# Feed-forward pass 0 of a hybrid decoder layer as one group of 1024 tokens

## The reference

```
hn2 = rmsnorm(x, norm2_g[l])
up, ffn_new = causal_dwconv(hn2 @ w_up[l], st_ffn[l], ffn_conv_w[l])
a_f, b_f = jnp.split(up, [D_FF], axis=-1)
x = x + (jax.nn.silu(a_f) * b_f) @ w_down[l]
y = rmsnorm(x, norm_f_g)
```

## Time and profile before

| | us |
|---|---|
| median of 3 timed runs | 3282.44 (3282.36 to 3284.39) |
| the profiled execution | 3280.0 |
| its span in the profile | 3278.3 |
| PE busy | 3182.3 |
| DVE busy | 2029.8 |
| ACT busy | 833.8 |
| POOL busy | 566.3 |
| feed-forward part, from PE's first product to the end | 1617.51 to 3278.3 |
| pass 1's first product | 2421.73 |

### The profile page before, as it was taken

The page is one execution under the profiler, slowest core; times in us unless marked ns, Lnnn a source line. Parts: engine busy times, 40 slices in busy tenths (PEclk is TensorE's granted clock), DMA queues, the critical chain, the costliest instruction groups (busy, mean ns, idle before and its releaser), DMA issues.

```text
span 3278.3 us, 56605 instructions
## 1 busy us (share of the span) xinstructions
PE 3182.3 (97%) x22353; PEld 2089.5 (64%) x22353; DVE 2029.8 (62%) x4678; ACT 833.8 (25%) x1743; POOL 566.3 (17%) x929
## 2 busy tenths in 40 slices
PE   7899999999999999996799999999998999999998
PEld 3555565566655565554577777777766766777765
DVE  1566665655566665665556666666675566666668
ACT  1223333233223333233321112211232221222213
POOL 1111110111111111112231111121053112111110
PEclk9999999999999999997799999999999999999999
DMA  7022222222222212215521111111133111111112
GB/s 241 11 82 85 85 65 85 85 64 66 66 78 85 85 66 84 80 54 162 168 80 39 52 52 39 39 52 39 39 124 117 39 52 41 50 39 39 43 35 78
DMA packets 223188, 236.37 MB, mean 72 GB/s; under 512 B 14204, under 2 KB 167332, under 8 KB 222931
## 3 DMA queue, kind: packets, MB, share of 16 engines
q1 hardware_dynamic: 222931, 232.81, 22.4%
HBM read 203.10 MB, written 29.67 MB: 71 GB/s over the span
## 4 chain that ended last, share of the span: by engine, by line
PE 49%; POOL 1%; issue 0%; DVE 0%; ACT 0%; DVEq 0%; POOLq 0%
PE mlp_bank L2131 32%; PE mlp_bank L2205 15%; PE mlp_bank L2219 2%; POOL acc L2453 0%; PE mlp_bank L2211 0%; POOL acc L2458 0%; DVE mcv L2573 0%; DVE acc L2634 0%; PE mlp_bank L2230 0%; ACT mcv L2294 0%; PE mlp_bank L2217 0%; ACT raw L2323 0%; ACT mth L2308 0%; DVE raw L2517 0%; POOL cf L2415 0%
## 5 line engine op out<-in xcount | busy, mean ns | idle before, releaser
L695 PE MATMUL mixer_bank<-arena,hnt 128*128 128x451 f32 x2048 | 864.1, 553 | 16.3 <-DMA arena<-in_w_in_dram 8.3
L2131 PE MATMUL mlp_bank<-arena,ws 128*128 128x256 f32 (+1 forms) x2816 | 648.3, 383 | 9.3 <-ACT raw L2321 9.3
L2131 PEld LDWEIGHTS mlp_bank<-arena,ws 128*128 128x128 f32 x2816 | 536.0, 190 | 92.6 <-ACT raw L2321 10.1
L695 PEld LDWEIGHTS mixer_bank<-arena,hnt 128*128 128x128 f32 x2048 | 366.1, 191 | 306.4 <-issue 301.4
L2205 PE MATMUL mlp_bank<-arena 128*128 128x512 f32 x1120 | 494.2, 593 | 0.0
L2606 DVE TENSOR_TENSOR acc<-acc,mlp_bank 128x512 f32<-128x512 f32 x560 | 370.2, 685 | 55.4 <-PE mlp_bank L2205 54.6
L2205 PEld LDWEIGHTS mlp_bank<-arena 128*128 128x128 f32 x1120 | 213.1, 190 | 234.7 <-issue 205.6
L645 POOL TENSOR_TENSOR ex<-dtt,level 128x512 f32<-128x512 f32 (+1 forms) x114 | 142.9, 1254 | 936.0 <-DVE dtt L1641 637.6
L2573 DVE SCALAR_TENSOR_TENSOR mcv<-raw,cf,mcv 128x512 f32<-128x512 f32 (+2 forms) x352 | 265.4, 770 | 59.2 <-ACT mcv L2294 50.3
L2131 PE MATMUL mlp_bank<-arena 128*128 128x256 f32 (+1 forms) x1056 | 249.4, 386 | 5.3 <-PEq L2716 4.3
L729 PE MATMUL mixer_bank<-wo,th 128*128 128x512 f32 x512 | 248.6, 608 | 2.7 <-DMA wo<-in_w_out_dram 2.1
(11 more groups left out here) (368 smaller groups left out, 3570.3 us busy)
## 6 DMA issues: line engine op xcount, KB each, us to landing
wo<-in_w_out_dram SPq DMA_DIRECT2D x260, 256.0 KB, 2.8
arena<-in_w_up_dram SPq DMA_DIRECT2D x44, 512.0 KB, 4.9
wu<-in_w_up_dram SPq DMA_DIRECT2D x44, 512.0 KB, 4.9
arena<-in_w_down_dram SPq DMA_DIRECT2D x40, 512.0 KB, 4.0
arena<-in_w_in_dram SPq DMA_DIRECT2D x7, 1804.0 KB, 16.2
xc<-in_x_t_dram SPq DMA_DIRECT2D x16, 512.0 KB, 4.1
xt<-in_x_prompt_dram SPq DMA_DIRECT2D x16, 512.0 KB, 5.0
xr<-in_x_prompt_dram SPq DMA_DIRECT2D x16, 512.0 KB, 3.8
```

The lines of the kernel that those rows point to most:

```text
L695: x = pe.matmul(bank[ring(g)][0:N, 0:GW], hnt[:, k, 0:N], w[:, k, g * GW:(g + 1) * GW], start=(k == 0), stop=(k == KT - 1))
L2131: x = pe.matmul(out[:, 0:N], left[:, k, :], xb[:, slot, k, g * N:(g + 1) * N], start=first and k == 0, stop=k == HK - 1, skip_group_check= ...
```

## The change

Pass 0 becomes one group of 1024 tokens. Its products have 512 columns. The run bank now alternates by block in pass 0 (`run_of`). `xb` slots are filled accordingly: the four early loads take the token columns in another order. All x sums of the whole width are needed by the first group, and `first_x_sums` moves to the head of POOL's queue. The convolution keeps pieces of 512 tokens, but both pieces of a block come behind the block's products, and on DVE behind the adds of the down half; on ACT the tanh of piece 0, the first taps of piece 1 and the tanh of piece 1 stand behind the copy of product 1 of the next block. In the last block of pass 0 piece 0 stands between the 7th and the 8th of the 14 adds. `half_block` counts pieces, `group` counts groups. Pass 1 does what it did.

```diff
-                    c0 = 2 * N0 * g + N0 * part
+                    c0 = 2 * N0 * part + N0 * g
...
-        PASSES = ((0, 2, 256, 0, 8), (T // 2, 2, 264, 8, 9))
-        J0 = (0, 2 * FT)
+        PASSES = ((0, 1, 512, 0, 8), (T // 2, 2, 264, 8, 9))
+        J0 = (0, FT)
+        WIDTH = (512, 528)
...
+        def run_of(ps, p, g):
+            return run_bank[g if ps else p]
...
-                    elif fixed(f, 1) and g == 1:
+                    elif fixed(f, 1):
                         pe.wait_ge(s_x1_made, 1)
...
                         m1_out(ps, f, p, 0)
                         if not fixed(f, 1):
-                            tanh(ps, f - 1, G - 1)
+                            if ps == 0:
+                                tanh(ps, f - 1, 0)
+                                first_taps(ps, f - 1, 1 - p, 1)
+                            tanh(ps, f - 1, 1)
...
+            first_x_sums()
             gp.memset(ident[:, :], 0.0).then_inc(s_ident_made, 1)
...
                     weight_sums(ps, 0, 0)
                     x_sums(ps)
-                else:
-                    first_x_sums()
...
-                return lambda: conv(ps, f, e, G - 1, 2 * p + e, i)
+
+                def rest(first=0 if ps == 0 else 1, last=2):
+                    for g in range(first, last):
+                        conv(ps, f, e, g, 2 * p + e, i)
+                return rest
...
-                last = up(ps, i, p, 0, (((), act_part), (first, second)))
+                last = up(ps, i, p, 0, (((), act_part), (first, second)) if ps else ((act_part + first, second),))
...
-                down(ps, i - 1, 1)
-                last()
+                if closing and ps == 0:
+                    down(ps, i - 1, 1, 0, 21)
+                    last(0, 1)
+                    down(ps, i - 1, 1, 7, 28)
+                    last(1, 2)
+                else:
+                    down(ps, i - 1, 1)
+                    last()
```

More of the change, by code:

```diff
@@ L2013, in two_before, with convolved @@
             if fixed(f, 2):
+                return 0 if ps == 0 else FT - 1 + f
+            return group(ps, f - 1, 0)
+        def convolved(ps, f):
+            if fixed(f, 2):
                 return 0 if ps == 0 else 2 * (FT - 1 + f)
-            return J0[ps] + PASSES[ps][1] * (f - 1)
+            return half_block(ps, f - 1, 0)
         def sums(engine, p, s_step, step, s_made):
@@ L2150, in up @@
                     J = group(ps, f, g)
-                    run = run_bank[g % 2]
+                    run = run_of(ps, p, g)
                     if g == 0:
@@ L2272, in m1_out @@
                 J = group(ps, f, g)
-                if g == 0 and two_before(ps, f) is not 0:
-                    act.wait_ge(s_act_made, two_before(ps, f))
+                if g == 0 and convolved(ps, f) is not 0:
+                    act.wait_ge(s_act_made, convolved(ps, f))
                     act.wait_ge(s_tails_kept, FT * ps + f - 1)
                 act.wait_ge(s_m1, J + 1)
-                act.copy(raw[p][0][:, c0:c0 + N], run_bank[g % 2][:, 0:N]).then_inc(s_m1_out, 1)
+                act.copy(raw[p][0][:, c0:c0 + N], run_of(ps, p, g)[:, 0:N]).then_inc(s_m1_out, 1)
             def first_taps(ps, f, p, g):
-                _, G, N, _, _ = PASSES[ps]
-                J = group(ps, f, g)
-                c0 = 2 * N * g
-                sample = ps == 1 and g == G - 1
-                n = 2 * N - S if sample else 2 * N
+                J = group(ps, f, g if ps else 0)
+                c0 = WIDTH[ps] * g
+                sample = ps == 1 and g == 1
+                n = WIDTH[ps] - S if sample else WIDTH[ps]
                 if g == 0:
@@ L2549, in conv @@
             def conv(ps, f, p, g, a, i):
-                _, G, N, _, _ = PASSES[ps]
-                J = group(ps, f, g)
-                c0 = 2 * N * g
-                sample = ps == 1 and g == G - 1
-                n = 2 * N - S if sample else 2 * N
+                J = group(ps, f, g if ps else 0)
+                K = half_block(ps, f, g)
+                W = WIDTH[ps]
+                c0 = W * g
+                sample = ps == 1 and g == 1
+                n = W - S if sample else W
                 if g == 0:
@@ L2595, in up, with down @@
                         conv(ps, f, e, g, 2 * p + e, i)
-                return lambda: conv(ps, f, e, G - 1, 2 * p + e, i)
-            def down(ps, i, half):
+                def rest(first=0 if ps == 0 else 1, last=2):
+                    for g in range(first, last):
+                        conv(ps, f, e, g, 2 * p + e, i)
+                return rest
+            def down(ps, i, half, first=0, last=0):
                 n = first_out(ps, i)
-                for o in range(14 * half, OUTS[ps] if half else 14):
+                for o in range(14 * half + first, min(last, OUTS[ps]) if last else (OUTS[ps] if half else 14)):
                     q, m = divmod(o, 7)
```

53 lines of the change are left out of this document (30 added, 23 removed).

## The result

| | before | after |
|---|---|---|
| median of 20 runs each | 3281.64 us (3279.28 to 3284.39) | 3288.60 us (3283.19 to 3293.04) |
| ratio, with its 95% interval | | 1.0023 [1.0016, 1.0029] |
| profiled execution, its span | 3280.0, 3278.3 us | 3289.32, 3287.2 us |

The change made the kernel 7.0 us slower. The forecast was +4.5 us (3286.9, counted from the first three runs of the kernel before, 3282.44) and a range of 3280 to 3294. The time lies in the range, but just over the 0.2% (6.6 us) up to which the forecast called it no change; 0.73 of its chance stood on the other side of that bound.

The account below looks back on a forecast made before the run. TensorE (PE) bounds the kernel, busy 3182.3 of 3278.3 us. Terms -3.1 + 2.0 + 0.4 + 0 + 0.8 + 4.4 = +4.5 us give 3286.9 against the timed median 3282.44, range 3280 to 3294.

Parts of the forecast that it names:

- Step 1: Blocks of pass 0: 56 instructions of 512 columns replace 112 of 256, 0.14 us saved in 22 blocks, -3.1 us.
- Step 2: Start of pass 0: PE's third product waits for x sums and weight sums while POOL and DVE take turns, +2.0 us.
- Step 3: Blocks 0 and 1: without down products to fill the gap, PE waits for a longer 512-column ACT copy, +0.4 us.
- Step 4: Steady blocks: ACT's queue still delivers the copy PE needs for its fifth product, with 2.5 us slack, 0 us.
- rival (b): Steady blocks: ACT's copy of product 3, behind two tanhs, comes after 13.7 us; 19 blocks lose 21 us; chance 0.07.
- Step 5: Block 2: old wait goes, but POOL's accumulator subtractions meet DVE's piece 1, a new 1.6 us wait; net +0.8 us.
- Step 6: Close of pass 0: PE's 10th down matmul waits for the 8th add behind piece 0, slowed by POOL's sums, +4.4 us.
- rival (c): Two longer waits of pass 0: the granted clock falls in each, about 2.4 us apiece, +9.3 in all; chance 0.07.
- (a): Stalls at start, block 2 and close: hidden because POOL and DVE miss each other, -0.7 us in all; chance 0.20.
- (d): Products of pass 0: 512 columns with accumulation cost more than plain ones, 5.3 us at 1%, 3292; chance 0.04.

Follow-up runs that it names:

- x4: Changed kernel with each 512-column product of pass 0 made as two of 256 columns: pass 0 814.12 us against 811.13, steady block 36.19 us.
- the padded kernels: Changed kernel with 3, 6 or 8 extra DVE operations ahead of piece 1's taps in blocks 2 to 20: pass 0 812.67, 833.50, 881.53 us.
- x2: Changed kernel with POOL making the x sums of the second 256 columns at the end of the program's first half: pass 0 809.29 us against 811.13.
- x12: Changed kernel with POOL's colliding work held back, x sums left at the head, and pass 1's accumulator prepared after block 2's tap copies: 3276.09 us, ratio 0.9984.
- x3: Changed kernel with POOL clearing and preparing pass 0's accumulator during block 0, not between blocks 1 and 2: pass 0 810.47 us against 811.13.
- x1: Changed kernel with POOL's weight sums for pass 1 held until piece 0 of block 21 is convolved: pass 0 809.49 us against 811.13.

## Why the prediction came near, and where it was off

Measured as the prediction counted (gaps with their refill):

| step | forecast | measured |
|---|---|---|
| 1, width | -3.1 | -3.1 (-2.7 read in blocks 3 to 21, the rest at their rate) |
| 2, start | +2.0 | +2.0 |
| 3, unfilled gaps | +0.4 | +0.6 |
| 4, ACT's queue | 0 | 0 in steady blocks, +0.65 in block 1 |
| 5, block 2 | +0.8 | +0.8 |
| 6, close | +4.4 | +4.1, and +1.8 of slow clock |
| sum | +4.5 | +6.9 |

**Step 1 was right**, by the blocks of 36.05 us and by x4.

**Step 2 was right, with its mechanism.** The third product began 11.25 us after the first, forecast 11.29. POOL and DVE after, at the start of pass 0, against rows 5 and 6:

```profile
1618.92 2.34 POOL L2413 TENSOR_TENSOR arena<-arena 128x1024 f32<-128x1024 f32 x1 [47.92 <-POOLq L2746]
...
1626.86 2.67 POOL L2418 TENSOR_TENSOR arena<-arena 128x1024 f32<-128x1024 f32 x1
```
```profile
1618.93 2.88 DVE L2035 TENSOR_TENSOR ws<-arena 128x512 f32<-128x512 f32 x1 [1.62 <-PEq L2746]
...
1627.36 2.72 DVE L2040 TENSOR_TENSOR ws<-arena,ws 128x512 f32<-128x512 f32 x1
```

The fourth DVE operation starts 8.43 us after the first, 2.8 for each of three steps, and POOL's 7.94, 2.65 each: the queues take turns. DVE's operations, 0.69 us alone, are stretched fourfold, and the pair ends at 10.6 (POOL) and 11.1 us (DVE) after the start. PE needs both and started at 11.25, so DVE's sums released it last, although its row names POOL. The rule weighed there, in SBUF — State Buffer, Who interferes with whom, of the Trainium skill (the first comer holds the shared port for its whole operation), agrees with these rows; the other reading, each engine only slowed, would have had DVE done 5.5 us after the start.

**Step 3** counted 0.2 per block for the longer copy; the gaps grew from 0.63 to 0.91 and 0.94 us.

**Step 4 was right for the 19 steady blocks**, and its slack was larger than said (3.3 us by the padded kernels, 2.5 forecast). ACT after, one steady block that begins at 2036.17, its second tanh and the copy behind it:

```profile
2045.50 0.63 ACT L2320 ACTIVATE mth<-mcv 128x512 f32<-128x512 f32 x1 [1.69 <-DVE mcv L2591]
...
2046.67 0.59 ACT L2336 COPY raw<-mlp_bank 128x512 f32<-128x512 f32 x1 [0.54 <-PE mlp_bank L2144]
```

The copy of product 3 starts 10.5 us after the block, forecast 10.6, and what it waits for last is PE's own product, not the tanh. The step failed in block 1, which I had given the same answer without working it out. There rival (b)'s chain did pass 13.7 us:

```profile
1652.60 1.28 ACT L2320 ACT_TABLE_LOAD   x1
...
1661.59 0.63 ACT L2320 ACTIVATE mth<-mcv 128x512 f32<-128x512 f32 x1 [2.47 <-DVE mcv L2591]
1662.12 0.57 ACT L2336 COPY raw<-mlp_bank 128x512 f32<-128x512 f32 x1
```

The copy ended 14.3 us after the block's start. A table load of 1.28 us stands ahead of block 1's first tanh, and POOL's weight sums for block 2, whose start a DMA set (x2), stretched the two DVE operations behind it to 1.51 and 1.64 us. x12 parts the two: its x sums stand at the head as in the changed kernel and its table load is in the same place, but POOL is held back past the collision:

```profile
1661.82 1.27 POOL L2035 TENSOR_TENSOR ws<-arena 128x512 f32<-128x512 f32 x1 [10.77 <-DVE arena L2614]
```

Its block 1 has no wait before the fifth product. So the meeting with POOL's weight sums is needed for the 0.65, and the table load alone makes none of it.

**Step 5 was right** in place, releaser and size: a wait of 1.31 us (1.47 with refill) on DVE's add, less the old one. x3 shows that the subtractions, with the clearing ahead of them, are the cause. The chain behind it was forecast as well: DVE's add was to end 23.9 us into the block and ended at 23.7.

**Step 6 is the step that was mis-sized**, +4.4 us for a place that cost 5.9. The wait came where the step had it, on the 8th add, 4.1 us against 4.4; of it 1.8 are turns with POOL (x1). DVE after, in the close; rows 9 have the undisturbed taps:

```profile
2391.46 4.77 DVE L2591 SCALAR_TENSOR_TENSOR mcv<-raw,cf,mcv 128x512 f32<-128x512 f32 x4
...
2397.48 3.20 DVE L2628 TENSOR_TENSOR acc<-acc,mlp_bank 128x512 f32<-128x512 f32 x5
```

Missing was a term for the granted clock: 1.8 us at the low level behind the wait. I had it as rival (c), with a chance of 0.07, a fall in both longer waits, and against it the waits of 0.5 us. These were no evidence for a wait eight times as long. The fall came behind one of the two waits only: after the start's wait of 1.7 us the next 24 instructions took 10.54, full speed.

**The rivals.** (a), all stalls hidden, is out: each of the three stalls came. (b) is out as a rule and true in one block. (c) is half right and is the larger part of the error: one fall of its two, at 1.8 us in place of 2.4. (d) is out. With +0.65, +1.8, +0.2 and -0.3 the forecast becomes +6.9. The misses hardly cancelled; the time stayed in the range because that was 14 us wide. Some nearness is luck: against the time itself (3288.60) the forecast is off by 1.7, against the change by 2.5, since the kernel before came out 0.8 below its first three runs. The chances also rested on a sum 2 us under the bound of 6.6 us: a small term left out was enough to pass it, and 0.24 for slower was too little.

**Open.** Why the clock falls at one wait of 2.2 us and not at the next, and why it stays low twice as long at one wait of 4 us as at another, is not settled; whether the close can be had without any wait was not tried (DVE is busy for 26.28 of 27.40 us behind it).

## What to carry to other kernels

When the bounding engine is to wait longer than before, add a possible stretch of slow clock to its price (here 1.8 or 3.1 us at a wait of 4 us, and 1.7 or nothing at one of 2.2), and take as evidence only waits of that length. When an operation with two inputs in SBUF is moved on POOL or DVE, look up what the other engine runs at its new time: here the pair cost about the sum of both, and moving it again only moves the meeting if a DMA sets its start. A saving per instruction that is small (0.6% of a product here) is worth less than one wait at either end of the loop, so look at the ends first, and at the largest wait of the bounding engine before any of them.
